# A gated-delta kernel: level 4 of the triangular inverse in 32x32 squares, two small steps moved by a quarter

## The reference, cut to what matters

```
M = beta[..., :, None] * einsum('bnhid,bnhjd->bnhij', k, k) * dec_strict
T = M + eye(chunk)
sol = solve_triangular(T, rhs, lower=True)      # rhs: [v*beta | k*beta*exp(bcum)]
u, w = sol[..., :DV], sol[..., DV:]
...
o = rms_norm(o, gdn_norm) * silu(z)
```

## Time and profile before

| what | us |
|---|---|
| median of 3 runs | 2887.7 |
| the profiled execution | 2882.68 |
| its span in the trace | 2881.0 |
| TensorE busy (PE) | 2796.5 (97%) |
| weight loads busy (PEld) | 2527.0 (88%) |
| VectorE busy (DVE) | 1473.1 (51%) |
| ScalarE busy (ACT) | 1000.4 (35%) |

### The profile page before, as it was taken

How to read it: one execution, slowest core, us unless ns; L and a number is a source line. 1 busy time by engine, 2 the same in 40 slices (tenths; PEclk the granted TensorE clock), 3 DMA queues, 4 the chain that set the end, 5 groups by cost and what they waited for, 6 DMA issues and landing times.

```text
span 2881.0 us, 39674 instructions
## 1 busy us (share of the span) xinstructions
PE 2796.5 (97%) x15928; PEld 2527.0 (88%) x15928; DVE 1473.1 (51%) x2151; ACT 1000.4 (35%) x1634; POOL 21.9 (1%) x59
## 2 busy tenths in 40 slices
PE   8999999999999999879999999999999999999998
PEld 7878888888888787779999998999999999999998
DVE  4666667766677556543333435433333445444343
ACT  3326556554655545422112113212112133222222
POOL 2000000000000000000000000000000000000000
PEclk9999999999999999989999999999999999999999
DMA  8355434434443484651222223421222242222220
GB/s 292 102 162 163 121 114 146 122 120 121 134 141 103 172 133 168 197 186 59 59 72 58 73 58 121 142 58 58 63 68 58 80 139 88 87 74 73 73 73 37
DMA packets 361875, 314.72 MB, mean 109 GB/s; under 512 B 15653, under 2 KB 315762, under 8 KB 359714
## 3 DMA queue, kind: packets, MB, share of 16 engines
q1 hardware_dynamic: 361762, 313.20, 36.5%
HBM read 254.80 MB, written 58.36 MB: 109 GB/s over the span
## 4 chain that ended last, share of the span: by engine, by line
PE 55%; DVE 1%; ACT 1%; issue 0%; DVEq 0%; POOL 0%; ACTq 0%; POOLq 0%
PE gate_ps L2524 6%; PE gate_ps L2526 6%; PE gate_ps L2525 6%; PE up_ps L2525 6%; PE up_ps L2526 6%; PE up_ps L2524 6%; PE down_ps L2525 6%; PE down_ps L2526 6%; PE down_ps L2524 6%; DVE w_in_sb L2518 0%; ACT h_hi L2320 0%; ACT w_hi L2301 0%; DVE w_in_sb L2419 0%; DVE h_lo L2441 0%; DVE w_in_sb L2463 0%
## 5 line engine op out<-in xcount | busy, mean ns | idle before, releaser
L1584 PE MATMUL pr_p<-hT_hi_p,w_hi_p 128*128 128x512 f32 x992 | 423.4, 427 | 6.8 <-DVE hT_lo_p L1050 4.5
L1586 PE MATMUL pr_p<-hT_hi_p,w_lo_p 128*128 128x512 f32 x992 | 393.1, 396 | 0.0
L1585 PE MATMUL pr_p<-hT_lo_p,w_hi_p 128*128 128x512 f32 x992 | 391.5, 395 | 0.0
L2405 DVE TENSOR_TENSOR w_in_sb<-up_ps,w_in_sb 128x384 f32<-128x384 f32 (+1 forms) x132 | 70.7, 536 | 605.4 <-PE up_ps L2526 605.4
L2524 PE MATMUL gate_ps<-h_hi,w_hi 128*128 128x384 f32 (+1 forms) x1056 | 346.3, 328 | 17.1 <-DVE w_lo L2395 14.4
L2526 PE MATMUL gate_ps<-h_hi,w_lo 128*128 128x384 f32 (+1 forms) x1056 | 345.8, 327 | 0.0
L2525 PE MATMUL gate_ps<-h_lo,w_hi 128*128 128x384 f32 (+1 forms) x1056 | 345.7, 327 | 0.0
L2524 PE MATMUL up_ps<-h_hi,w_hi 128*128 128x384 f32 (+1 forms) x1056 | 344.0, 326 | 0.0
L2525 PE MATMUL up_ps<-h_lo,w_hi 128*128 128x384 f32 (+1 forms) x1056 | 343.9, 326 | 0.0
L2526 PE MATMUL up_ps<-h_hi,w_lo 128*128 128x384 f32 (+1 forms) x1056 | 343.9, 326 | 0.0
L2419 DVE TENSOR_TENSOR w_in_sb<-down_ps,w_in_sb 128x1024 f32<-128x1024 f32 x187 | 228.7, 1223 | 183.1 <-PE down_ps L2526 182.2
(11 more groups left out here) (366 smaller groups left out, 4418.7 us busy)
## 6 DMA issues: line engine op xcount, KB each, us to landing
w_in_sb<-in_w_in SPq DMA_DIRECT2D x100, 512.0 KB, 4.3
w_in_sb<-in_w_gate SPq DMA_DIRECT2D x66, 512.0 KB, 4.0
w_in_sb<-in_w_up SPq DMA_DIRECT2D x66, 512.0 KB, 5.2
w_in_sb<-in_w_down SPq DMA_DIRECT2D x33, 1024.0 KB, 4.9
stream_tiles<-w_in_sb SPq DMA_DIRECT2D x96, 256.0 KB, 2.5
w_in_sb<-stream_tiles SPq DMA_DIRECT2D x16, 1280.0 KB, 7.6
w_in_sb<-mixed_tiles SPq DMA_DIRECT2D x29, 512.0 KB, 5.1
out<-w_in_sb SPq DMA_DIRECT2D x21, 512.0 KB, 3.6
```

Source lines behind the costliest of these rows:

```text
L1584: pe.matmul(out, w_h, x_h, start=start, stop=False)
L1585: pe.matmul(out, w_h, x_l, start=False, stop=False)
L1586: return pe.matmul(out, w_l, x_h, start=False, stop=stop)
L2405: dve.tensor_tensor(act[:, h, 0:half], up_ps[h][:, 0:half], gate_act[:, h, 0:half], ALU.mult)\
```

## The change

Three parts.

1. Level 4 works in squares of 32 by 32: of each block of 64 rows (n = 0, 1) the even rows are the first 32, the odd ones the next 32 (`quadrants()`). Each of the three products of a head is two matmuls with 32x32 weights and 32 moving columns, in place of one with 128x128 weights and 64 moving columns, which computed products of zeros as well. VectorE's updates of X and of XT are two instructions each, on 32 partitions and 4x32 elements.
2. `output_norm(t)` on TensorE moves from quarter 24 to the end of the slot.
3. `gates_sums(j)` on VectorE moves from behind quarter 15 to behind quarter 14 (l = 2).

The diff, without the new helper for names of views in PSUM (`of_heads`):

```diff
@@ VectorE, level @@
-                    even = halves(X[:], l, 0)
-                    dve.tensor_tensor(even, even, half_bank(gb[1], l), ALU.subtract).then_inc(s["x_new"], 1)
+                    if l == SMALL:
+                        for n, even, odd in quadrants():
+                            last = dve.tensor_tensor(X[odd, :, even], X[odd, :, even], of_heads(gb[1], n)[odd], ALU.subtract)
+                        last.then_inc(s["x_new"], 1)
+                    else:
+                        even = halves(X[:], l, 0)
+                        dve.tensor_tensor(even, even, half_bank(gb[1], l), ALU.subtract).then_inc(s["x_new"], 1)
...
+                    for n, even, odd in quadrants():
+                        part = XT[even, :, odd]
+                        last = dve.tensor_tensor(part, part, of_heads(gb[2], n)[even], ALU.subtract)
@@ VectorE, slot @@
                     if t >= 0:
                         level(l, t)
+                    if l == 2 and (t + MACRO) % MACRO == 1 and j < MACROS:
+                        gates_sums(j)
                     upto(t, 11 + 2 * l)
...
-                    if l == 2 and (t + MACRO) % MACRO == 1 and j < MACROS:
-                        gates_sums(j)
@@ TensorE, level_lx @@
+                    if l == SMALL:
+                        for n, even, odd in quadrants():
+                            last = pe.matmul(of_head(gb[0], h_)[odd, n * QP:(n + 1) * QP], lt[even, l % 2, h_, odd],
+                                             X[even, h_, even], start=True, stop=True)
+                    elif l == LV - 1:
@@ TensorE, level_xlx @@
+                        if l == SMALL:
+                            for n, even, odd in quadrants():
+                                last = pe.matmul(of_head(gb[1], h_)[odd, n * QP:(n + 1) * QP], XT[odd, h_, odd],
+                                                 LX[l][odd, h_, even], start=True, stop=True)
...
-                        last = pe.matmul(of_head(gb[2], h_), LX[l][:, h_], halves(XT[:, h_:h_ + 1], l, 1),
-                                         start=True, stop=True)
+                    for n, even, odd in quadrants():
+                        last = pe.matmul(of_head(gb[2], h_)[even, n * QP:(n + 1) * QP], LX[l][odd, h_, even],
+                                         XT[odd, h_, odd], start=True, stop=True)
@@ TensorE, slot @@
+                upto(t, SLOT)
                 if t >= 0:
-                    upto(t, 24)
                     output_norm(t)
-                upto(t, SLOT)
```

More of the change, by code:

```diff
@@ L161, in prompt_phase @@
     HC = D_MODEL // 2
-    HP = P // 2
+    HP, QP = P // 2, P // 4
     wo_dram = a["w_o"].rearrange("(c p) n -> p c n", p=P)
@@ L366, in half_bank, with quadrants, of_heads @@
             return bank_[:, 0:W // 2].rearrange("p (n r) -> p n r", r=2 << l)
+        def quadrants():
+            return [(n, slice(n * HP, n * HP + QP), slice(n * HP + QP, (n + 1) * HP)) for n in range(2)]
+        def of_heads(bank_, n=None):
+            x = bank_[:, 0:W // 2].rearrange("p (h r) -> p h r", h=H_B)
+            return x if n is None else x[:, :, n * QP:(n + 1) * QP]
         def over_heads(mask):
@@ L1453, in level @@
                 dve.wait_ge(s["xT_new"], levels(t, l - 1))
-                rows = slice(0, HP) if l == LV - 1 else slice(0, P)
-                odd = halves(XT[:], l, 1)[rows]
-                dve.tensor_tensor(odd, odd, half_bank(gb[2], l)[rows], ALU.subtract).then_inc(s["xT_new"], 1)
+                if l == LV - 1:
+                    part = XT[0:HP, :, HP:]
+                    last = dve.tensor_tensor(part, part, of_heads(gb[2])[0:HP], ALU.subtract)
+                else:
+                    for n, even, odd in quadrants():
+                        part = XT[even, :, odd]
+                        last = dve.tensor_tensor(part, part, of_heads(gb[2], n)[even], ALU.subtract)
+                last.then_inc(s["xT_new"], 1)
             def gmlp(t):
@@ L1910, in level_lx @@
                 for h_ in range(H_B):
-                    if l == LV - 1:
+                    if l == SMALL:
[3 more added lines that the diff above has]
+                    elif l == LV - 1:
                         last = pe.matmul(of_head(gb[0], h_)[HP:], lt[0:HP, l % 2, h_, HP:], X[0:HP, h_, 0:HP],
@@ L1928, in level_xlx @@
                     for h_ in range(H_B):
-                        last = pe.matmul(of_head(gb[1], h_), XT[:, h_], halves(LX[l][:, h_:h_ + 1], l, 0),
-                                         start=True, stop=True)
+                        if l == SMALL:
+                            for n, even, odd in quadrants():
+                                last = pe.matmul(of_head(gb[1], h_)[odd, n * QP:(n + 1) * QP], XT[odd, h_, odd],
+                                                 LX[l][odd, h_, even], start=True, stop=True)
+                        else:
+                            last = pe.matmul(of_head(gb[1], h_), XT[:, h_], halves(LX[l][:, h_:h_ + 1], l, 0),
+                                             start=True, stop=True)
                     last.then_inc(s["xlx_pe"], 1)
@@ L1937, in level_xlx @@
                                          start=True, stop=True)
-                    else:
-                        last = pe.matmul(of_head(gb[2], h_), LX[l][:, h_], halves(XT[:, h_:h_ + 1], l, 1),
-                                         start=True, stop=True)
+                        continue
+                    for n, even, odd in quadrants():
+                        last = pe.matmul(of_head(gb[2], h_)[even, n * QP:(n + 1) * QP], LX[l][odd, h_, even],
+                                         XT[odd, h_, odd], start=True, stop=True)
                 last.then_inc(s["xlxT_pe"], 1)
```

## The result

The changed kernel takes 2868.45 us (median of 4 runs, 2866.32 to 2877.37) against 2888.5 us beside it. The ratio is 0.9939 with an interval of 0.9926 to 0.9952, so 17.6 us less (13.9 to 21.4), where 6.6 less was forecast. The recorded ratio is not the quotient of these two medians, which lie 20.1 us apart; where this text says "us less" of a run, it goes by the ratio.

What follows compares the result with a forecast made beforehand. TensorE was taken to bound the prompt phase. Level 4's -8.2, +1.4 taken back, and the norm's -1.4 and +1.6 summed to -6.6 us, 2881.1 us from the median 2887.7; range 2875 to 2899.

Steps and rivals of the forecast that it cites:

- each pass 0.031 us: Level 4 on TensorE: price of a 32x32 pass, on the line through 0.111 and 0.058 us; saves 8.2 us in all.
- The case: Level 4: neighbouring squares may overlap, or waits behind the norm shrink; -10 to -13 us, 2876 us, chance 0.10.
- nothing to be told from below: Level 4: a 32x32 pass costs at most 0.058 us, with no lower bound but the two changes of shape.
- The change of shape: Level 4: going to another shape of weights and back costs 0.35 us, paid twice a tile, at lx and the pair.
- The rival on the other side: Level 4: small passes are not cheaper, 0.058 us or more each since issuing sets the pace; +12.1, 2899.8 us, chance 0.22.
- Taken back at tiles 2, 6 and 10: Level 5: TensorE waits for ACT's copy of LX, so the pair's 0.45 us returns three times, +1.4 us.
- VectorE's split updates: Level 4: each update gets longer by 0 to 0.42 us, covered before level 5 needs X; 0, uncovered up to 13 us.
- The norm: Output norm one quarter later: -1.4 us at tile 13, +1.6 at tiles 2 and 6, otherwise 0.
- tile 13's 1.4: Output norm at tile 13: its 1.44 us gap is filled and the time kept, since ACT's chain has room; -1.4 us.
- up to +1.4: Output norm at tile 12: 0 expected, possibly this much loss, as a store of y stands ahead of weight loads on SP.
- The gates' sums: Sums one quarter sooner on VectorE, which stands 1.12 us for TensorE before the next update either way; 0.
- the +1.6: Output norm at tiles 2 and 6: its later result delays the next tile's level-2 update by 0.79 us each.

Runs made afterwards that it cites:

- e4: The changed kernel with the loops over heads and squares exchanged in level 4's three products; 2878.89 us, ratio 0.9974 to the kernel before the change.
- e2: The kernel before the change with only the output norm moved one quarter later; 2886.41 us against 2886.06, ratio 1.0002.
- e3: The kernel before the change with only the gates' sums moved one quarter sooner; 2883.63 us against 2886.06, ratio 0.9996.

## Why the prediction was wrong, point by point

- **The step that failed** is the one that turned "each pass 0.031 us" into "sixteen passes 16 x 0.031". The price of a pass at its own place was right: rounds start 0.032 us apart. But two squares of a head lie at two places, and their passes run in pairs: 8 x 0.031 + 0.35 = 0.60 for lx (predicted 0.85, measured 0.57), and for the pair, whose products lap over each other, 0.73 (predicted 1.34), where four places in full would give 0.60. So 1.38 a tile in place of 0.51, -22.1 in place of -8.2. The trace of before has nothing but one place at a time, so it could not show an overlap, and I took its absence for evidence. e4 shows that it is the overlap: with neighbours at one place the same passes cost 0.44 us a tile more. The case stood among the rivals with a chance of 0.10 and was priced at -10 to -13 for the whole change, where the sum put right below is -18.7.
- **The bound "nothing to be told from below"** was stated and then not kept: a pass was bounded by 0.058 from above and by nothing from below, and the range's low end, 2875 or -12.7 in all, goes with a pass of about 0.023. It should have reached to a pass of zero, 2.69 - 0.69 = 2.0 us a tile, 32 us. The point estimate itself, drawn through two points (0.111 and 0.058), held: 0.032 at one place in e4.
- **The change of shape**, 0.35 us twice a tile: right (0.34 and 0.39).
- **The rival on the other side**, passes at 0.058: no. The floor of about 25 ns under any spacing, from the Trainium skill's "TensorE: Matmul & The Clock Gate", section "Wait — 56ns, not 53.3ns?", does not hold between passes at different places, which start 0.014 us apart on the mean. What the Trainium skill says in "TensorEngine Tiling (Array Packing)", Key Properties, that tiles at different positions can load and run in parallel, is what these traces show.
- **Taken back at tiles 2, 6 and 10**: the place was right. Three times the pair's own saving is 3 x 1.06 = 3.2; in the trace 3.5 us (L1964), where it had been 0.4.
- **VectorE's split updates** at no cost: right. Two instructions of 0.287 us overlap and take 0.57 to 0.59 us together, some 0.15 more than the one of 0.42, and no wait at level 5 hangs on them.
- **The norm**: the sum (+0.2) fits the times (e2: no difference within 0.1%), its parts only in part, so the sum owes something to luck. Tiles 3, 7 and 11 gave back at hT_lo as described (4.5 to 8.8 us), tiles 3 and 7 wait at level 2. Wrong: tile 13's 1.4 is not kept, and tile 11 has a wait at level 2 as well (0.58 us in e2, 0.94 in the changed kernel). At tile 12, where up to +1.4 was allowed, e2 has 1.24 more, but e3 shows that this wait moves by as much and more without the norm.
- **The gates' sums**: right, nothing.
- **Not in the prediction**: the longer waits at tile 12 (2.4 to 3.0 us, not shown to come from the change) and those of tiles 13 to 15 behind transfers. With the one size put right, -22.1 + 3.2 - 1.4 + 1.6 = -18.7, inside the measured interval of the first measurement (-13.9 to -21.4); the -1.4 and the +1.6 are kept as forecast, though of them only the sum is borne out.

## What to carry to other kernels

Small matmuls whose weights use 32 rows and 32 columns are priced by the place, not by the number: in these traces each place takes a pass about every 0.03 us, with 16 moving columns as with 32, four places (the most that was tried) run at once, and the change of shape costs some 0.35 us once per group. So order them so that neighbours lie at different places, put products that share a shape into one group, and pay the change of shape once. A wait that is removed from an engine is worth nothing until one has followed it to the next wait of the same engine; here 8.7 us went, and the time did not change. And before a longer wait is put down to a change, look at it in a run without the change: tile 12's was 6.25 us in one.

## What the runs showed that was not expected

- Passes at different places start 6 or 7 ns apart within a pair or a round of four (14 on the mean over a group of pairs), and a later product's matmuls start before the earlier product's have all started (707.18 against 707.20 above).
- The time of one and the same kernel moves by 11 us, together with the granted clock: 2864.6 us at 0.990 to 2875.7 at 0.985. In the profiled execution the clock stood at 1.2 GHz from 128.5 to 142.2 us, in a part of the program that the change does not touch:

```profile
128.50:142.20 13.70, 13.70 (x53) 12.44 (x53) 1.89 (x6) 2.81 (x6) 0.00 (x0) 0.50 0.07 19
```

  The kernel before has 6.8 us of it there; that alone is 3.4 us of difference between the two profiles. Elsewhere waits and the clock go together: in the trace of before, seven of the twelve stretches at 1.2 GHz start 0.3 to 1.7 us after TensorE has ended a wait of 1.6 to 4.0 us (at 344.17, 402.78, 586.18, 644.79, 880.51, 972.54 and 1048.43), so such a wait can cost more than its own length.
- A correction to the section on the kernel: level l joins blocks of 2<<l rows, so level 4 joins blocks of 32 to 64 and level 5 the tile's two blocks of 64 to one of 128.
